# Interleaving the high and low weight halves, and running the moving operand and the sums of TensorE back to front

## The reference

```python
proj = h @ w_in
...
mix = jnp.concatenate([o_a, o_s], axis=-1) @ w_out
x = x + rms_norm(mix, post_mix_norm)
...
u = causal_dwconv(h @ w_up, ffn_conv_w, ffn_conv_b)
gate, up = jnp.split(u, 2, axis=-1)
f = (jax.nn.silu(gate) * up) @ w_down
```

## Time and profile before

| | |
|---|---|
| median of 3 runs | 2150.36 us (2149.61 to 2154.43) |
| profiled execution | 2149.57 us, span of the core 2147.8 us |
| mean granted TensorE clock | 0.995 |
| TensorE matmuls | 9776, busy 98% |
| TensorE weight loads | 9776, busy 79% |
| VectorE / ScalarE / GpSimd busy | 56% / 42% / 15% |
| HBM read and written | 187.7 MB, 87 GB/s |

### The profile page before, as it was taken

How to read it: one execution, slowest core, us unless ns; L and a number is a source line. 1 busy time by engine, 2 the same in 40 slices (tenths; PEclk the granted TensorE clock), 3 DMA queues, 4 the chain that set the end, 5 groups by cost and what they waited for, 6 DMA issues and landing times.

```text
span 2147.8 us, 26841 instructions
## 1 busy us (share of the span) xinstructions
PE 2098.5 (98%) x9776; PEld 1699.6 (79%) x9776; DVE 1212.0 (56%) x1663; ACT 906.0 (42%) x1282; POOL 326.6 (15%) x266
## 2 busy tenths in 40 slices
PE   6999999999999999999999999999999999999999
PEld 4778888878868888887766888888868878888887
DVE  5898755765366666225544566653354465666522
ACT  5883445434244444224564444442242354444411
POOL 0001221220112222001301122220000012222200
PEclk9999999999999999999999999999999999999999
DMA  7323222122212223222211232332222122222321
GB/s 235 94 75 96 82 77 71 49 69 73 95 67 94 93 96 120 95 82 67 69 40 49 89 98 98 98 114 94 86 69 88 60 73 94 98 98 97 115 95 66
DMA packets 81481, 188.96 MB, mean 88 GB/s; under 512 B 19824, under 2 KB 40432, under 8 KB 81392
## 3 DMA queue, kind: packets, MB, share of 16 engines
q1 hardware_dynamic: 81392, 187.75, 26.9%
HBM read 178.28 MB, written 9.44 MB: 87 GB/s over the span
## 4 chain that ended last, share of the span: by engine, by line
PE 92%; DVE 4%; ACT 2%; issue 1%; DMA 0%; POOL 0%; SPq 0%; DVEq 0%; ACTq 0%
PE acc L256 23%; PE acc L258 23%; PE acc L257 23%; PE bank L1248 1%; PE bank L232 1%; PE bank L1730 1%; PE bank L234 1%; PE bank L233 1%; PE acc L2636 1%; PE acc L2637 1%; PE acc L2638 1%; PE bank L2021 1%; PE bank L256 1%; PE bank L258 1%; PE bank L257 1%
## 5 line engine op out<-in xcount | busy, mean ns | idle before, releaser
L256 PE MATMUL acc<-HH,whi 128*128 128x512 f32 x1600 | 644.1, 403 | 6.8 <-DVE wlo L194 4.3
L258 PE MATMUL acc<-HH,wlo 128*128 128x512 f32 x1600 | 626.2, 391 | 0.0
L257 PE MATMUL acc<-HL,whi 128*128 128x512 f32 x1600 | 625.3, 391 | 0.0
L188 ACT ACTIVATE whi<-raw 128x1024 fp32r<-128x1024 f32 (+1 forms) x293 | 324.1, 1107 | 567.0 <-PE acc L258 537.7
L194 DVE TENSOR_TENSOR wlo<-raw,whi 128x1024 fp32r<-128x1024 f32 (+1 forms) x293 | 399.7, 1365 | 283.3 <-ACT whi L188 283.3
L256 PEld LDWEIGHTS acc<-HH,whi 128*128 128x128 f32 x1600 | 302.1, 189 | 73.8 <-DVE wlo L194 9.5
L258 PEld LDWEIGHTS acc<-HH,wlo 128*128 128x128 f32 x1600 | 301.5, 188 | 64.8
L257 PEld LDWEIGHTS acc<-HL,whi 128*128 128x128 f32 x1600 | 302.3, 189 | 62.5 <-issue 4.1
L256 PE MATMUL acc<-FH,whi 128*128 128x512 f32 x528 | 205.8, 390 | 0.0
L257 PE MATMUL acc<-FL,whi 128*128 128x512 f32 x528 | 205.4, 389 | 0.0
L258 PE MATMUL acc<-FH,wlo 128*128 128x512 f32 x528 | 205.4, 389 | 0.0
(11 more groups left out here) (393 smaller groups left out, 2666.8 us busy)
## 6 DMA issues: line engine op xcount, KB each, us to landing
raw<-w SPq DMA_DIRECT2D x257, 512.0 KB, 3.5
raw<-w SPq DMA_DIRECT2D x48, 704.0 KB, 3.9
X<-x SPq DMA_DIRECT2D x4, 512.0 KB, 5.4
x_dram<-small SPq DMA_DIRECT2D x8, 256.0 KB, 4.3
xt_dram<-small SPq DMA_DIRECT2D x8, 256.0 KB, 3.7
a_dram<-l_am SPq DMA_DIRECT2D x8, 256.0 KB, 3.4
l_xt<-xt_dram SPq DMA_DIRECT2D x8, 256.0 KB, 3.3
l_x<-x_dram SPq DMA_DIRECT2D x8, 256.0 KB, 3.2
```

The costliest lines, as they stand in the source:

```text
L188: nc.scalar.activation(hi[:, 0:kt * P], raw[u % RAW][:, 0:kt * P], ACT.Copy).then_inc(w_hi_ready, 1)
L256: nc.tensor.matmul(a[:, :], wh, tile(hi, k), start=start and k == 0, stop=False)
L257: nc.tensor.matmul(a[:, :], wh, tile(lo, k), start=False, stop=False)
L258: last = nc.tensor.matmul(a[:, :], wl, tile(hi, k), start=False, stop=stop and k == kt - 1)
```

## The change

The high and the low half of the weights go word by word into one buffer: word 2i is high, word 2i + 1 is low. There are two such buffers, for even and odd units, and the second starts 128 bytes further modulo 512. `whi` and `wlo` become views with a step of two words. ScalarE writes every second word, VectorE reads every second word and writes the ones between, and TensorE loads its 128 weights from every second word of 1024 bytes.

The helper `back` gives a 512-column tile in reverse order. All float32r passes of the weights read the moving operand through it and write their sums through it, so that the sums land where they did. Plain float32 matmuls, and the passes of `busy`, keep their order. The number of instructions on each engine stays.

```
+WEIGHTS_AT = (0, 128)
...
-        whi = [fixed(f"whi{j}", [P, HALF * P], F32R) for j in range(SPLIT)]
-        wlo = [fixed(f"wlo{j}", [P, HALF * P], F32R) for j in range(SPLIT)]
+        split = []
+        for shift in WEIGHTS_AT:
+            top[0] += (base_w + shift - top[0]) % LINE
+            split.append(fixed(f"split{len(split)}", [P, 2 * HALF * P], F32R))
+
+        def high_low(t, n):
+
+            return t[:, 0:2 * n:2], t[:, 1:2 * n:2]
+
+        whi, wlo = zip(*(high_low(t, HALF * P) for t in split))
...
-        first_weights = {}
+        first_weights, first_split = {}, {}
...
+            first_split[at0] = [place(f"first{at0}_{j}", 2 * KD * P, FREE + (at0 + 4 * j) * TILE, F32R) for j in range(2)]
+            first_weights[at0] = [high_low(t, KD * P) for t in first_split[at0]]
...
+        def back(t, k=0):
+
+            return t[:, (k + 1) * S - 1:k * S - 1 if k else None:-1]
...
-                nc.tensor.matmul(a[:, :], wh, tile(hi, k), start=start and k == 0, stop=False)
-                nc.tensor.matmul(a[:, :], wh, tile(lo, k), start=False, stop=False)
-                last = nc.tensor.matmul(a[:, :], wl, tile(hi, k), start=False, stop=stop and k == kt - 1)
+                nc.tensor.matmul(back(a), wh, back(hi, k), start=start and k == 0, stop=False)
+                nc.tensor.matmul(back(a), wh, back(lo, k), start=False, stop=False)
+                last = nc.tensor.matmul(back(a), wl, back(hi, k), start=False, stop=stop and k == kt - 1)
...
-            busy(c["spare"][0], c["first"][0][0], 18)
+            busy(c["spare"][0], c["first_split"][0], 18)
```

More of the change, by code:

```diff
@@ L125, in program @@
         assert FREE + 2 * KF * TILE <= TMP
-        first_weights = {}
+        first_weights, first_split = {}, {}
         for at0 in (0, 8, 16):
-            first_weights[at0] = [tuple(place(f"first_{n}{at0}_{j}", KD * P, FREE + (at0 + 4 * j + 2 * m) * TILE, F32R)
-                                        for m, n in enumerate(("hi", "lo"))) for j in range(2)]
+            first_split[at0] = [place(f"first{at0}_{j}", 2 * KD * P, FREE + (at0 + 4 * j) * TILE, F32R) for j in range(2)]
+            first_weights[at0] = [high_low(t, KD * P) for t in first_split[at0]]
         acc = [ctx.enter_context(nc.psum_tensor(f"acc{j}", [P, S], F32)) for j in range(2)]
@@ L231, in fan @@
                     a, (wh, wl) = c["spare"][j], (x[:, k * P:(k + 1) * P] for x in w[j])
-                    nc.tensor.matmul(a[:, :], wh, tile(hi, k), start=k == 0, stop=False)
-                    nc.tensor.matmul(a[:, :], wh, tile(lo, k), start=False, stop=False)
-                    last = nc.tensor.matmul(a[:, :], wl, tile(hi, k), start=False, stop=k == KD - 1)
+                    nc.tensor.matmul(back(a), wh, back(hi, k), start=k == 0, stop=False)
+                    nc.tensor.matmul(back(a), wh, back(lo, k), start=False, stop=False)
+                    last = nc.tensor.matmul(back(a), wl, back(hi, k), start=False, stop=k == KD - 1)
                     if k == KD - 1:
@@ L276, in program @@
         NARROW = 32
-        early = [tuple(place(f"early_{n}{j}", KD * P, FREE + (24 + 4 * j + 2 * m) * TILE, F32R)
-                       for m, n in enumerate(("hi", "lo"))) for j in range(2)]
+        early = [high_low(place(f"early{j}", 2 * KD * P, FREE + (24 + 4 * j) * TILE, F32R), KD * P) for j in range(2)]
         tab_w = place("tab_w", KD * NARROW, FREE + 17 * TILE)
@@ L1312, in sb_pe @@
             pe.wait_ge(w_lo_ready, u0 + 12)
-            busy(bank[0], whi[(u0 + 11) % SPLIT], 12)
+            busy(bank[0], split[(u0 + 11) % SPLIT], 12)
             for i in range(NP):
@@ L1467, in begin_pe @@
                         pe.wait_ge(w_lo_ready, m + 1)
-                    nc.tensor.matmul(a[:, :], wh, tile(HH, k), start=k == 0, stop=False)
-                    nc.tensor.matmul(a[:, :], wh, tile(HL, k), start=False, stop=False)
-                    last = nc.tensor.matmul(a[:, :], wl, tile(HH, k), start=False, stop=k == KD - 1)
+                    nc.tensor.matmul(back(a), wh, back(HH, k), start=k == 0, stop=False)
+                    nc.tensor.matmul(back(a), wh, back(HL, k), start=False, stop=False)
+                    last = nc.tensor.matmul(back(a), wl, back(HH, k), start=False, stop=k == KD - 1)
                     if k == KD - 1:
@@ L2635, in mix_pe @@
                     wh, wl = whi[w][:, j * P:(j + 1) * P], wlo[w][:, j * P:(j + 1) * P]
-                    nc.tensor.matmul(a[:, :], wh, tile(hi, j), start=h == 0 and j == 0, stop=False)
-                    nc.tensor.matmul(a[:, :], wh, tile(lo, j), start=False, stop=False)
-                    last = nc.tensor.matmul(a[:, :], wl, tile(hi, j), start=False, stop=h == 1 and j == KD - 1)
+                    nc.tensor.matmul(back(a), wh, back(hi, j), start=h == 0 and j == 0, stop=False)
+                    nc.tensor.matmul(back(a), wh, back(lo, j), start=False, stop=False)
+                    last = nc.tensor.matmul(back(a), wl, back(hi, j), start=False, stop=h == 1 and j == KD - 1)
                 last.then_inc(unit_done, 1)
@@ L2691, in program @@
                 c["spare"], c["first"] = [bank[b] for b in SPARE[kind]], first_weights[at0]
+                c["first_split"] = first_split[at0]
                 stages[-2][2]["next_first"] = first_weights[at0]
```

## The result

The changed kernel takes 2198.06 us (median of 4 runs, 2194.62 to 2200.59) against 2150.79 us before (4 runs): ratio 1.0216, 95% interval 1.0195 to 1.0237. It is 47 us slower. I had forecast 2077 us.

The account below looks back on a forecast made before the run. TensorE's price per pass was taken to bound the kernel: 7752 passes at 226.7 ns. Gaining 11 ns each gave 61 us steady plus 12 us mixed, 73 us off 2149.6, so 2077 us; range 2058 to 2185 us.

Parts of the forecast that it names:

- What bounds the kernel: Whole kernel: TensorE's price per pass bounds it; 7752 weight passes at 226.7 ns are 1757 us, 82% of the span.
- 13.4 ns without columns: Each float32r weight pass: 226.7 ns start to start less 213.3 ns for 512 columns; 104 us in all.
- the control: Passes of `busy`, still in forward order, were to stay at 226.7 ns in the changed kernel's trace.
- two reads of SBUF getting into each other's way: Each weight pass: weight load and moving read said to collide, costing 11.8 of the 13.4 ns; marked as an inference.
- The comparison with plain float32 passes (1.6 ns): Plain float32 matmuls of 512 columns, each with a weight load, take 428.3 ns, only 1.6 ns above their columns.
- the lockstep of the sweeps: Weight load and moving read would both advance 8 bytes a step, at one speed, and might keep a fixed distance.
- the 11 ns to win: Gain taken per weight pass, nearly all of 11.8 ns: 61 us on steady passes, 12 us on mixed ones.
- A term that the sum put at nothing: Reading and writing in reverse on TensorE's weight passes: taken as free, since neighbouring words stay neighbours.
- The distance between the sweeps: Set by odd units' 128 bytes; if sweeps run the same way they meet always or never, up to 107 ns a pass.
- Rival "nothing changes": The 13.4 ns belong to float32r's swap of weights, not to addresses; time 2150 us; chance 0.12.
- Rival "reverse is taken word by word": Each of 7752 passes costs 201.6 ns more, 428.3 ns, up to 3713 us in all; chance 0.12.
- Splits: ScalarE's and VectorE's writes and reads of every second word: 0 for both engines; doubling would add 16 us.

Follow-up runs that it names:

- extra passes: Kernel before plus rows of 13 passes that nobody reads, differing in start, step, direction and columns, behind the attention stage's `busy` passes; priced per pass, no whole time given.

## Why the prediction was wrong

**What bounds the kernel** held: the span followed the price of a pass, 47 us for 7752 passes that are 6.7 ns dearer (52 us). 226.7 ns, 13.4 ns without columns, and 104 us as their whole were read rightly, and the control (L234 unchanged) behaved as said.

**The failing step** is "I read 13.4 - 1.6 = 11.8 ns as two reads of SBUF getting into each other's way". With this term the sum took 11 ns off each pass; in the run each pass became 6.7 ns dearer. The runs show that the surplus is not the time of the load's words: a load of 32 columns, 108 ns long instead of 188, leaves a pass at 231.5 ns, and with the moving operand in reverse at 233.1 ns. The load is not without a say, since the start and the step of the weights alone move the price with the moving operand forward. The comparison with plain float32 passes (1.6 ns) misled me: they differ from float32r in the rate of the moving read as well as in the room for a load, and I took the second. All that followed, the lockstep of the sweeps and the 11 ns to win, rests on this step. A term that the sum put at nothing failed as well: reading in reverse costs 6.7 ns at 512 columns. Weights with a step of two words, which were to bring part of the gain, cost 6.7 ns by themselves. The distance between the sweeps has no say in reverse: weights 4 and 32 words on gave the same 233.1 ns.

**Below 226.7 ns** nothing was found except a moving operand that repeats one to four words (218.5 to 220.0 ns). The figure of the Trainium skill's "TensorE: Matmul & The Clock Gate", section "Back-to-back issue gap" (about 216 ns), was the mean of no row here; the rows come within 3 to 4 ns of it only when the moving operand repeats a few words. That section gives the figure for an isolated matmul, which the prediction left out, and 131 ns at 512 columns for a stream of loads and matmuls, which no row here comes near. I had used the 216 ns, with the row of the float32 passes, as what could be won.

**Rival "nothing changes"** had the better view of the cause, that the surplus doesn't come from the length of the load. The two independent read ports of the Trainium skill's "TensorE: Matmul & The Clock Gate", section "Part 2: What happens when you issue a matmul", fit the rows with smaller loads. It had the wrong consequence: that the layout can't matter. It can make the pass dearer, by start (weights 128 bytes further, +5.7 ns), by step (+6.7) and by direction (+6.7). That all buffers start at the same place modulo 512 I took as "speaks neither way"; it meant that the kernel before had a good place to lose.

**Rival "reverse is taken word by word"** had the right sign and the wrong size: reverse costs 6.7 ns, not 201.6. The rule of the Trainium skill's "PSUM — Partial Sum Buffer", "Specifications (TRN2)", on access patterns that aren't contiguous does not show in reversed sums beside neighbouring weights: 233.3 ns with them and without. I gave this rival the price of a rate; at 512 columns reverse costs 6.7 ns, at 256 columns nothing.

**Splits.** For VectorE 0 was right (1228 against 1226 ns). ScalarE's 0 was wrong by 114 ns, some 75 of them by the step alone, without consequence: TensorE waited for splits 16.3 us, before 16.4.

**Open.** Why a start, a step or a direction costs 5.7 to 6.7 ns is not shown, only that it sits with the reads and, for the direction, that it is there at 512 columns and gone at 256. What the 13.4 ns are stays open too. Nor is it shown what switches passes of one layout between 233.3 and 236.7 ns: in the changed kernel even units are dear in the up stages of layers one and two and not in that of layer three, and without the 128 bytes layers one and three are dear and layer two is not. The extra passes, which overwrite a bank instead of adding to it, never showed it.

## What to carry to other kernels

Before building on a mechanism that two instruction types seem to show, shrink the suspected party: a row of extra passes with a 32-column load would have refuted mine for 3 us of device time. Where a kernel's hot operands all stand at one alignment, its trace can't say what alignment is worth; assume that there is something to lose, and try each edit of start, step and order alone. Before a difference of 3 ns a pass is put down to a layout, look at other stages and other executions of the same kernel: here one layout had both prices. In this kernel float32r passes were cheapest with weights side by side, weights and moving operand a multiple of 256 bytes apart, and forward reads: 226.7 ns for 512 columns was the least that real data reached.

## What the runs showed of the hardware

- A float32r pass carries 12.5 to 13.8 ns above its columns at 2.4 GHz with 256, 384 or 512 columns (15.6 and 18.5 ns with 448 and 504). With 64 or 32 weight columns instead of 128 it is no cheaper (230.0 and 231.5 against 226.7 ns).
- 7 to 8 of these ns go when the moving operand repeats up to 4 words (218.5 to 220.0 ns); repeating 16 words is dearer (241.5) than reading 512 different ones. The Trainium skill's "SBUF — State Buffer", section "Door 1: The DMA port swizzle", speaks of 16-byte lines, 4 such words; the rows have an edge somewhere between 4 and 16 words, which doesn't show that it is this line.
- A moving operand in reverse costs 6.7 ns a pass of 512 columns and nothing at 256 (118.5 against 119.2 ns); one with a step of two words costs 226 ns more (453 ns), weights with a step of two 6.7 ns.
- Weights 128 bytes further cost 5.7 ns a pass in the whole kernel (232.4 against 226.7 ns), 256 bytes further nothing.
- Passes of one code and layout can run at either of two steady prices in different stages of one execution (236.7 and 233.3 ns in the run without the 128 bytes).
- ScalarE's writes with a step of two words had medians of 1133 and 1136 ns over all splits instead of about 1060, and 1175 to 1186 where TensorE also read in reverse; VectorE's low splits stayed at 1226 to 1229.
